# Weight columns interleaved by 2, 4, 8 or 11 chunks, and tokens read from the last to the first, in a two-layer block on one core

## What is computed

```python
h = modulate(rmsnorm(x, norm1_g[i]), shift1, scale1)
z = h @ w_in[i] + b_in[i]
...
x = x + gate1[:, None, :] * (y @ w_out[i])
h2 = modulate(rmsnorm(x, norm2_g[i]), shift2, scale2)
g_ff, up_ff = jnp.split(h2 @ w_ffn_in[i], 2, axis=-1)
x = x + gate2[:, None, :] * ((jax.nn.silu(g_ff) * up_ff) @ w_ffn_out[i])
```

## The kernel before

| stage | lines | us from start | matmuls |
|---|---|---|---|
| w_in | 1172-1174, 383-385 | 50 to 188 | 384 |
| w_out | 1172-1174 | 188 to 247 | 192 |
| ffi0 | 400-402, 383-385 | 247 to 495 | 1056 |
| ffo0 | 383-385 | 496 to 617 | 528 |
| att5 | 1368-1370, 383-385 | 617 to 682 | 120 |
| att6 | 1437-1439 | 682 to 875 | 384 |
| att_out | 1437-1439 | 876 to 951 | 192 |
| ffi1 | 383-385 | 977 to 1206 | 1008 |
| ffo1 | 383-385 | 1206 to 1326 | 528 |
| ffi2 | 383-385 | 1390 to 1619 | 1008 |
| ffo2 | 383-385 | 1619 to 1739 | 528 |

## Time and profile before

### The profile page before, as it was taken

How to read it: one execution, slowest core, us unless ns; L and a number is a source line. 1 busy time by engine, 2 the same in 40 slices (tenths; PEclk the granted TensorE clock), 3 DMA queues, 4 the chain that set the end, 5 groups by cost and what they waited for, 6 DMA issues and landing times.

```text
span 1757.1 us, 22185 instructions
## 1 busy us (share of the span) xinstructions
PE 1679.6 (96%) x8263; PEld 1311.8 (75%) x8263; DVE 916.1 (52%) x1376; ACT 627.2 (36%) x946; POOL 225.3 (13%) x204
## 2 busy tenths in 40 slices
PE   1999899999999999999999999999998999999996
PEld 1757688888888867666667788888887688888885
DVE  6765676544334463666667544444336644444223
ACT  1324334222223362554555333333226333333221
POOL 5010106998000030000000000003000000000000
PEclk9999999999999999999998999999999899999998
DMA  7565134454332241111101322233211133333221
GB/s 281 204 200 167 40 110 161 169 181 157 109 107 97 69 117 64 37 37 49 37 25 61 108 96 95 95 100 115 98 57 49 61 98 100 99 96 115 92 80 48
DMA packets 48588, 179.27 MB, mean 102 GB/s; under 512 B 5968, under 2 KB 6640, under 8 KB 48272
## 3 DMA queue, kind: packets, MB, share of 16 engines
q1 hardware_dynamic: 43600, 162.04, 27.5%
q0 software_dynamic: 3776, 14.78, 2.7%
q10 hardware_dynamic: 1152, 1.66, 0.4%
HBM read 173.04 MB, written 2.10 MB: 100 GB/s over the span
## 4 chain that ended last, share of the span: by engine, by line
PE 71%; issue 22%; DVE 5%; DMA 1%; ACT 1%; ACTq 1%; POOL 0%; POOLq 0%; DVEq 0%; SPq 0%
PE bank L383 15%; PE bank L385 14%; PE bank L384 14%; PE bank L1437 3%; PE bank L1439 2%; PE bank L1438 2%; PE bank L1545 2%; PE bank L1501 2%; PE bank L1521 2%; DVE ada_acc L1972 1%; PE bank L1172 1%; PE bank L1174 1%; PE bank L1173 1%; PE bank L454 1%; PE bank L1394 1%
## 5 line engine op out<-in xcount | busy, mean ns | idle before, releaser
L309 DVE TENSOR_TENSOR w_lo<-raw,w_hi 128x1024 fp32r<-128x1024 f32 (+1 forms) x229 | 316.4, 1382 | 575.2 <-ACT w_hi L305 574.9
L305 ACT ACTIVATE w_hi<-raw 128x1024 fp32r<-128x1024 f32 (+1 forms) x229 | 258.0, 1127 | 564.4 <-PE bank L385 482.7
L383 PE MATMUL bank<-h_hi,w_hi 128*128 128x512 f32 x1136 | 448.0, 394 | 0.5 <-DVE w_lo L309 0.5
L385 PE MATMUL bank<-h_hi,w_lo 128*128 128x512 f32 x1136 | 442.2, 389 | 0.0
L384 PE MATMUL bank<-h_lo,w_hi 128*128 128x512 f32 x1136 | 442.2, 389 | 0.0
L383 PEld LDWEIGHTS bank<-h_hi,w_hi 128*128 128x128 f32 x1136 | 213.2, 188 | 50.2 <-issue 5.2
L385 PEld LDWEIGHTS bank<-h_hi,w_lo 128*128 128x128 f32 x1136 | 213.2, 188 | 45.0
L384 PEld LDWEIGHTS bank<-h_lo,w_hi 128*128 128x128 f32 x1136 | 213.3, 188 | 44.6 <-issue 1.7
L383 PE MATMUL bank<-hid_hi,w_hi 128*128 128x512 f32 x528 | 205.6, 389 | 0.0
L384 PE MATMUL bank<-hid_lo,w_hi 128*128 128x512 f32 x528 | 205.4, 389 | 0.0
L385 PE MATMUL bank<-hid_hi,w_lo 128*128 128x512 f32 x528 | 205.4, 389 | 0.0
(11 more groups left out here) (397 smaller groups left out, 2079.5 us busy)
## 6 DMA issues: line engine op xcount, KB each, us to landing
raw<-in_f2i SPq DMA_DIRECT2D x88, 512.0 KB, 3.3
raw<-in_ffi SPq DMA_DIRECT2D x44, 512.0 KB, 3.4
raw<-in_f2o SPq DMA_DIRECT2D x32, 704.0 KB, 4.0
ada_w<-in_ada_w SPq DMA_DIRECT2D x24, 512.0 KB, 4.3
m_out<-in_ada_w POOLq DMA_DIRECT2D x24, 512.0 KB, 3.7
raw<-in_att_w SPq DMA_DIRECT2D x23, 512.0 KB, 3.3
raw<-in_ffo SPq DMA_DIRECT2D x16, 704.0 KB, 4.0
raw<-in_ada_w SPq DMA_DIRECT2D x16, 512.0 KB, 4.9
```

The source lines that it names most:

```text
L305: nc.scalar.activation(WH[par][:, 0:kc * P], RAW[s][:, 0:kc * P], ACT.Copy).then_inc(whi, count)
L309: nc.vector.tensor_tensor(WL[par][:, 0:kc * P], RAW[s][:, 0:kc * P], WH[par][:, 0:kc * P].bitcast(F32), ALU.subtract).then_inc(wlo, count)
L383: pe_.matmul(bank[:, :], w_h, hi[:, k0 + k, :], start=start and k == 0, stop=False)
L385: last = pe_.matmul(bank[:, :], w_l, hi[:, k0 + k, :], start=False, stop=stop and k == kc - 1)
```

## The change

The host lays the weights out in another way and TensorE reads them accordingly. `MIX` gives for each stage a number r and a flag. Of each r chunks of a block (or of what is left at its end) the columns are interleaved in memory: column c of chunk k lies at place c*r + k%r of the group. `wcols` takes the 128 columns of chunk k back with a step of r elements of 4 bytes. The same columns meet the same tokens as before. Where the flag is set, `turned` gives the 512 tokens of the moving operand and the 512 places of the bank in descending order (a step of -1), so that each result lands where it did.

By the table the step is 1 in att5; 2 in ffi0, att_out, ffi1 and ffo2; 4 in w_in and att6; 8 in w_out and ffi2; 11 in ffo0 and ffo1. Tokens run backwards in w_out, att6, ffi1, ffo1 and ffo2. The sums over shift vectors and the float32 chunks take the interleaved weights too, without the reversal. Transfers, splits and evacuations are as they were: they handle whole blocks and whole banks. Every engine has the same instructions in the same order, with the same waits; only operand patterns of TensorE and line numbers differ.

```diff
 CHUNKS = (1, 0, 2, 3)
+MIX = {"w_in": (4, False), "w_out": (8, True), "ffi0": (2, False), "ffo0": (11, False), "att5": (1, False), "att6": (4, True),
+       "att_out": (2, False), "ffi1": (2, True), "ffo1": (11, True), "ffi2": (8, False), "ffo2": (2, True)}
...
-        def block(n, par, kc, hi, lo, k0, bank, start, stop, ready=None, between=None):
+        def wcols(tile, k, name, kc=C):
+
+            r = min(MIX[name][0], kc - k // MIX[name][0] * MIX[name][0])
+            at = k // MIX[name][0] * MIX[name][0] * P
+            return tile[:, at + k % MIX[name][0]:at + r * P:r]
+
+        def turned(ap, name):
+            return ap[:, ::-1] if MIX[name][1] else ap
+
+        def block(name, n, par, kc, hi, lo, k0, bank, start, stop, ready=None, between=None):
 
             pe_ = nc.tensor
+            out = turned(bank[:, :], name)
             pe_.wait_ge(wlo, n + 1)
             for k in range(kc):
                 if ready is not None:
                     pe_.wait_ge(n_lo, ready + k + 1)
-                w_h, w_l = WH[par][:, k * P:(k + 1) * P], WL[par][:, k * P:(k + 1) * P]
-                pe_.matmul(bank[:, :], w_h, hi[:, k0 + k, :], start=start and k == 0, stop=False)
-                pe_.matmul(bank[:, :], w_h, lo[:, k0 + k, :], start=False, stop=False)
-                last = pe_.matmul(bank[:, :], w_l, hi[:, k0 + k, :], start=False, stop=stop and k == kc - 1)
+                w_h, w_l = wcols(WH[par], k, name, kc), wcols(WL[par], k, name, kc)
+                x_h, x_l = turned(hi[:, k0 + k, :], name), turned(lo[:, k0 + k, :], name)
+                pe_.matmul(out, w_h, x_h, start=start and k == 0, stop=False)
+                pe_.matmul(out, w_h, x_l, start=False, stop=False)
+                last = pe_.matmul(out, w_l, x_h, start=False, stop=stop and k == kc - 1)
                 if between is not None and k < kc - 1:
                     between(k)
...
                     for e, w in enumerate((WH[t], WL[t])):
-                        m = pe_.matmul(PS[2][:, 2 * t:2 * t + 2], w[:, k * P:(k + 1) * P], SHL[:, k, :],
+                        m = pe_.matmul(PS[2][:, 2 * t:2 * t + 2], wcols(w, k, name), SHL[:, k, :],
...
-                    m = pe_.matmul(PS[2 + t][:, :], RAW[t][:, k * P:(k + 1) * P], XG[:, k, :], start=k == 0,
+                    m = pe_.matmul(PS[2 + t][:, :], wcols(RAW[t], k, name), XG[:, k, :], start=k == 0,
...
-                w_h, w_l = WH[t][:, k * P:(k + 1) * P], WL[t][:, k * P:(k + 1) * P]
-                pe_.matmul(PS[t][:, :], w_h, hi[:, k, :], start=first, stop=False)
-                pe_.matmul(PS[t][:, :], w_h, lo[:, k, :], start=False, stop=False)
-                m = pe_.matmul(PS[t][:, :], w_l, hi[:, k, :], start=False, stop=last)
+                w_h, w_l, out = wcols(WH[t], k, name), wcols(WL[t], k, name), turned(PS[t][:, :], name)
+                x_h, x_l = turned(hi[:, k, :], name), turned(lo[:, k, :], name)
+                pe_.matmul(out, w_h, x_h, start=first, stop=False)
+                pe_.matmul(out, w_h, x_l, start=False, stop=False)
+                m = pe_.matmul(out, w_l, x_h, start=False, stop=last)
...
+def _mixed(w, name):
+
+    b, p, n = w.shape
+    r, kc = MIX[name][0], n // P
+    full = kc // r * r
+    parts = [w[:, :, :full * P].reshape(b, p, full // r, r, P).transpose(0, 1, 2, 4, 3).reshape(b, p, full * P)]
+    if full < kc:
+        parts.append(w[:, :, full * P:].reshape(b, p, kc - full, P).transpose(0, 1, 3, 2).reshape(b, p, (kc - full) * P))
+    return np.concatenate(parts, axis=2)
...
-        "w_in": np.concatenate(order), "w_out": _blocks(a["w_out"][0]), "ffi": gu(f[:CF], f[CF:]),
+        "w_in": _mixed(np.concatenate(order), "w_in"), "w_out": _mixed(_blocks(a["w_out"][0]), "w_out"),
+        "ffi": _mixed(gu(f[:CF], f[CF:]), "ffi0"),
+        "ffo": _mixed(_down(a["w_ffn_out"][0]), "ffo0"), "ln_rows": np.stack([a["a_ln_g"][0], a["a_ln_b"][0]]),
...
```

More of the change, by code:

```diff
@@ L395, in up @@
                 nc.tensor.wait_ge(ev[t % 2], cnt + 2 * g + t // 2)
-                block(n + 4 * g + t, t % 2, C, hi, lo, 0, PS[t % 2], True, True)
+                block(name, n + 4 * g + t, t % 2, C, hi, lo, 0, PS[t % 2], True, True)
             def part(t, w, h_, l_, k):
[L399 to L402, removed]
+                w_h, w_l, out = wcols(WH[w], k, name), wcols(WL[w], k, name), turned(PS[t][:, :], name)
+                x_h, x_l = turned(h_[:, k, :], name), turned(l_[:, k, :], name)
+                pe_.matmul(out, w_h, x_h, start=k == 0, stop=False)
+                pe_.matmul(out, w_h, x_l, start=False, stop=False)
+                return pe_.matmul(out, w_l, x_h, start=False, stop=k == C - 1)
             def shift_sums(t):
@@ L461, in pe_phase_renewed @@
                 pe_.wait_ge(ev[t % 2], O0[name] // 2)
-                block(n + t, t % 2, C, HH, HL, 0, PS[t % 2], True, True, q.lo)
+                block(name, n + t, t % 2, C, HH, HL, 0, PS[t % 2], True, True, q.lo)
             with nc.tensor.Fori(1, G[name]) as g:
@@ L465, in pe_phase_renewed @@
                     pe_.wait_ge(ev[t % 2], O0[name] // 2 + 2 * g + t // 2)
-                    block(n + 4 * g + t, t % 2, C, HH, HL, 0, PS[t % 2], True, True)
+                    block(name, n + 4 * g + t, t % 2, C, HH, HL, 0, PS[t % 2], True, True)
         def pe_down(name, hid_ready, behind_first=None):
@@ L473, in down @@
                 nc.tensor.wait_ge(hid_ready, KH * (t % 2 + 1))
-                block(N0[name] + 4 * g + t, t % 2, KH, FH, FL, KH * (t % 2), PS[t // 2],
+                block(name, N0[name] + 4 * g + t, t % 2, KH, FH, FL, KH * (t % 2), PS[t // 2],
                       t % 2 == 0, t % 2 == 1)
@@ L1168, in _, with part @@
             ada_sums(1, PS[5], raw_used, 2 * C)
-            def part(t, k, hi, lo, first, last):
-                w_h, w_l = WH[t][:, k * P:(k + 1) * P], WL[t][:, k * P:(k + 1) * P]
-                pe_.matmul(PS[t][:, :], w_h, hi, start=first, stop=False)
-                pe_.matmul(PS[t][:, :], w_h, lo, start=False, stop=False)
-                return pe_.matmul(PS[t][:, :], w_l, hi, start=False, stop=last)
+            def part(name, t, k, hi, lo, first, last):
+                w_h, w_l, out = wcols(WH[t], k, name), wcols(WL[t], k, name), turned(PS[t][:, :], name)
+                x_h, x_l = turned(hi, name), turned(lo, name)
+                pe_.matmul(out, w_h, x_h, start=first, stop=False)
+                pe_.matmul(out, w_h, x_l, start=False, stop=False)
+                return pe_.matmul(out, w_l, x_h, start=False, stop=last)
             def first_two():
@@ L1183, in first_two @@
                         k = step - LAG
-                        m = part(1, k, HH[:, k, :], HL[:, k, :], k == 0, k == C - 1)
+                        m = part("w_in", 1, k, HH[:, k, :], HL[:, k, :], k == 0, k == C - 1)
                     if step < C:
@@ L1189, in first_two @@
                         pe_.wait_ge(n_lo, nj["n1"].lo + step + 1)
-                        m0 = part(0, step, HH[:, step, :], HL[:, step, :], step == 0, step == C - 1)
+                        m0 = part("w_in", 0, step, HH[:, step, :], HL[:, step, :], step == 0, step == C - 1)
                         if step == C - 1:
@@ L1199, in out_part @@
                 hi, lo = out_chunk(k)
-                return part(t, k, hi, lo, k == CA, k == CA - 1)
+                return part("w_out", t, k, hi, lo, k == CA, k == CA - 1)
             def out_block(n):
@@ L1298, in _ @@
                 pe_.wait_ge(ev[n % 2], n // 2 + 1)
-                block(n, n % 2, C, HH, HL, 0, PS[n % 2], True, True, None, lambda k: inside(n, k))
+                block("w_in", n, n % 2, C, HH, HL, 0, PS[n % 2], True, True, None, lambda k: inside(n, k))
                 if n in (5, 7, 9):
@@ L1363, in lin @@
                 pe_.wait_ge(ev[t % 2], O0[name] // 2 + 2 * g + t // 2)
-                block(N0[name] + 4 * g + t, t % 2, C, HH, HL, 0, PS[t % 2], True, True, ready, between)
+                block(name, N0[name] + 4 * g + t, t % 2, C, HH, HL, 0, PS[t % 2], True, True, ready, between)
             def att_part(w, low, k):
[L1367 to L1370, removed]
+                w_h, w_l, out = wcols(WH[w], k, "att5"), wcols(WL[w], k, "att5"), turned(PS[w][:, :], "att5")
+                x_h, x_l = turned(HH[:, k, :], "att5"), turned(low[:, k, :], "att5")
+                pe_.matmul(out, w_h, x_h, start=k == 0, stop=False)
+                pe_.matmul(out, w_h, x_l, start=False, stop=False)
+                return pe_.matmul(out, w_l, x_h, start=False, stop=k == C - 1)
             n5, cnt5 = N0["att5"], O0["att5"] // 2
@@ L1383, in _ @@
                 for half, w_ in enumerate((WH[0], WL[0])):
-                    m = pe_.matmul(PS[2][:, 0:2], w_[:, k * P:(k + 1) * P], FSH[:, k, :], start=k == 0 and half == 0,
+                    m = pe_.matmul(PS[2][:, 0:2], wcols(w_, k, "att5"), FSH[:, k, :], start=k == 0 and half == 0,
                                    stop=k == C - 1 and half == 1, skip_group_check=True)
```

(4 more changed lines are left out.)

10 lines of the change are left out of this document (5 added, 5 removed).

## The result

The changed kernel takes 1838.22 us (median of 2 runs, 1837.79 to 1838.64) against 1760.57: ratio 1.0443, 95% interval 1.0412 to 1.0473. It is slower by 78 us, outside the range of 1752 to 1830. The span grew from 1757.1 to 1836.9 us.

The account below looks back on a forecast made before the run. The prediction took the kernel to be bound by a line of TensorE matmuls 0.226 us apart. Only exposed stepped loads added time: 1760.6 + 11.6 = 1772 us, range 1752 to 1830.

Parts of the forecast that it names:

- Nothing but TensorE is touched: Whole kernel: no instruction added, removed or moved; other engines and queues do the same work, costed at nothing.
- A stepped load lasts longer: Weight loads at steps 4, 8 and 11: +100 ns for 128 columns, so 288 ns instead of 188.
- A stepped load should then allow a start every 0.11 + 0.10 = 0.21 us ... In a dense stretch the load still fits: Dense stages, steps 4, 8, 11: overlapping loads stay hidden under matmuls 0.226 us apart, by 5 to 15 ns.
- rival 1: Dense stages above step 2: load becomes the pace by 5 to 15 ns, 15 to 45 us more, 1787 to 1817; chance 0.11.
- Step 2 at a price of 0: Weight loads in the step 2 stages, 2784 matmuls: costed at 0, as nearest to adjacent columns.
- Reversal at nothing: Reversed tokens in w_out, att6, ffi1, ffo1, ffo2, 2640 matmuls: costed at nothing, same columns from the far end.
- Rival 3: Reversed stages: a reversed row goes at half speed, 0.45 us a matmul, 591 us more, near 2360; chance 0.11.
- Exposed loads, 11.6 us: att6, w_in, w_out: 82, 26 and 8 first loads without a 512-token matmul over them, 116 x 0.10 us.

Follow-up runs that it names:

- first set: Bare-matmul kernel computing nothing of the reference, 64 matmuls in a row per form of weights, tokens or bank: 0.2267 us apart at step 1, 0.256 at step 11.

## Why the prediction was wrong

- *Nothing but TensorE is touched*: right. No instruction moved, the other engines kept their busy times, and single stages pay for themselves (ffi2 and ffo2 alone).
- *A stepped load lasts longer*: right in kind, too small in size. I put 288 ns; att6 (step 4) has 309, ffi2 (step 8) 327 to 329, ffo0 (step 11) 346 to 349.
- *"A stepped load should then allow a start every 0.11 + 0.10 = 0.21 us ... In a dense stretch the load still fits"*: this is the step that failed. The sum used 23 ns on the 31 columns of `ke` and scaled it to 128. Measured alone, a load stands 0.233 us from the next at step 4, 0.238 at 8 and 0.247 at 11: 122 to 135 ns above step 1, where I had 100. That is over 0.226, so the loads became the pace, by 7 ns and more. This was rival 1, to which I gave 0.11, with 5 to 15 ns; the kernel shows 7 to 9 at step 4, 18 to 21 at step 8 and 26 to 27 at step 11. Why `ke` had looked cheaper is open; a step of 32 with 128 columns and 512 tokens stands at 0.237, so the size of the step is not all of it. Nor is the type: `ke` is plain float32, and in plain float32 a load of 128 columns lasts 313 ns at step 8 and 190 at step 1 (first set).
- *Step 2 at a price of 0*: wrong, and the second step that failed. Its load alone takes 6 ns more and would fit, yet the matmuls stand 6.7 ns further apart. ffi0, att_out, ffi1 and ffo2 lose 18 us by it. I had argued from the even distance that tokens and weights don't hinder each other. The even 0.2267 was one value among several (0.2267 to 0.2366) that places in SBUF give.
- *Reversal at nothing*: wrong by itself (+14.4 us alone), right in this change by luck, where each reversed stage also has a step above 1 and the two don't add up. Of the two halves only reading costs; the bank written backwards is free. Rival 3 wanted 0.45 us for a reversed row; it is 0.2333.
- *Exposed loads, 11.6 us*: att6 was to give 82 x 0.10 = 8.2 and gave 10.2, the rest of its 11.1 being mostly dense distance; the run with att6 alone is 10.8 us longer than before. The count of 82 held, at 0.12 us each. w_in and w_out have 13 and 6 such places, fewer than the 26 and 8 of the forecast, so with a higher price the whole term came out at 12 us, near its size, partly by luck.
- Sum: steps above 2 in w_in, w_out, ffo0, att6, ffo1 and ffi2 make 63 us, step 2 makes 18, att5 took 1 less: 80. Of the 63, some 52 are dense distance and 12 exposed loads. I had 12 in all, and nothing for the dense distance.
- The range ended at 1830 because it took rival 1 at 5 to 15 ns for all steps alike, and a step of 2 at nothing. Steps of 8 and 11, three quarters of the 3024 matmuls concerned, cost 18 to 27 ns. The 63 us alone would have given 1824 and stayed inside; with the 18 us of step 2 the time left the range.
- The Trainium skill (Advanced Engine Details and Errata, "SBUF Cachelines") says that at least two hits on a 16-byte line are needed for full speed. The load alone agrees: 0.112 and 0.118 us at steps 1 and 2, 0.233 at 4. Beside 512 tokens a step of 2 is not free: 0.2333 us against 0.2267.

## What to carry to other kernels

Where a load hides behind a matmul with a margin of a few per cent, measure the load's own pace (two token columns, clock held up by dense matmuls) at the very step before counting on the cover; a price scaled from a smaller load was 18 to 26% too low, and that was more than the margin. Keep the weight columns of one fp32r piece adjacent and its tokens ascending: a step of 2 or a reversed row costs 3% of dense time, a step of 4 costs 4%, 8 and 11 cost 8 to 12%. An even distance between matmuls does not show that their reads are independent.

## What the runs showed of the hardware that was not expected

- A load's pace by step, alone: 0.112, 0.118, 0.175, 0.233, 0.238, 0.247 us for 1, 2, 3, 4, 8, 11. In the first set, at half the granted clock, steps 4, 8 and 11 gave the same 0.233, 0.238 and 0.247.
- The distance of fp32r matmuls of 512 tokens depends on where weights and tokens start relative to each other, 0.2267 to 0.2366 us at step 1.
- Reading tokens at steps 2, 3, 4 and 8 takes 0.43 to 0.46 us for 512; reading them backwards 0.2333; writing the bank backwards nothing.
- ffi1 with the same table entry (step 2, reversed) ran at 0.2333 us in the changed kernel and at 0.2367 in two others, at the same clock; this stays open.
- In plain float32 a load at step 8 lasts 313 ns instead of 190 too, but there it stays hidden: the passes stand 0.429 us apart at either step (first set).
